# Attention over 16 heads: values as stationary operand in 64-column groups, two heads at a time

## The reference, cut to what matters

```python
def attend(q, k, v):                                   # 16 heads, dk 96, dv 64
    ...
    s = jnp.einsum('bqhd,bkhd->bhqk', qblk, k).astype(jnp.float32) * scale
    p = jax.nn.softmax(s, axis=-1).astype(v.dtype)
    return jnp.einsum('bhqk,bkhd->bqhd', p, v)
# o -> (tokens, 16*64) @ a_wo, times sigmoid(gate), added to the merged branches
```

## Time and profile before

| | |
|---|---|
| Median of 3 runs | 2784.48 us (2783.02 to 2785.2) |
| Profiled execution, its own time | 2785.75 us |
| Its span in the trace | 2783.9 us |
| Busy: TensorE, VectorE, ScalarE, GpSimd | 88%, 32%, 18%, 4% |
| Weight loads (beside the matmuls) | 54% |
| Mean granted TensorE clock | 0.927 of full |
| DMA | 440.60 MB, 158 GB/s over the span |

### The profile page before, as it was taken

One profiled execution on the slowest core, in us unless ns is written; L12 is line 12 of the kernel. 1 busy time (PEld: TensorE's weight loads), 2 busy tenths in 40 slices (PEclk: granted clock), 3 DMA queues, 4 the chain that ended last, 5 costly groups with the idle time before them and its releaser, 6 DMA issues. The chain is left out here.

```text
span 2783.9 us, 39618 instructions
## 1 busy us (share of the span) xinstructions
PE 2454.4 (88%) x16902; PEld 1508.4 (54%) x16902; DVE 893.8 (32%) x1492; ACT 510.1 (18%) x906; POOL 106.0 (4%) x74
## 2 busy tenths in 40 slices
PE   6999999889899969999479999997898999599893
PEld 3546654554576545555245476555545765455552
DVE  2255312431558130000113562224315661300002
ACT  1133202210223021010021241022102220201000
POOL 0000000000021000000000000001001110000000
PEclk8999999899989979999789999898999899699996
DMA  6321132114314277999353201411243222799972
GB/s 241 106 93 61 54 140 93 46 61 151 125 32 146 91 297 272 376 373 345 115 184 112 93 31 62 165 61 46 71 159 117 89 78 91 298 346 379 375 272 80
DMA packets 162338, 440.60 MB, mean 158 GB/s; under 512 B 10150, under 2 KB 50086, under 8 KB 153448
## 3 DMA queue, kind: packets, MB, share of 16 engines
q1 hardware_dynamic: 144360, 412.75, 40.6%
q10 hardware_dynamic: 14336, 12.59, 1.5%
q0 software_dynamic: 3456, 12.58, 1.2%
HBM read 400.38 MB, written 37.52 MB: 157 GB/s over the span
## 5 line engine op out<-in xcount | busy, mean ns | idle before, releaser
L293 PE MATMUL ps<-space 128*128 128x384 f32 (+3 forms) x1696 | 475.5, 433 | 14.9 <-DVE space L469 8.5
L293 PE MATMUL ps<-hT,space 128*128 128x384 f32 x1344 | 461.3, 504 | 27.3 <-ACT hT L407 12.1
L293 PEld LDWEIGHTS ps<-space 128*128 128x128 f32 x1696 | 300.1, 194 | 187.7 <-issue 48.4
L293 PEld LDWEIGHTS ps<-hT,space 128*128 128x128 f32 x1344 | 262.0, 197 | 213.4 <-issue 41.4
L1673 PE MATMUL ps<-space 128*32 128x256 f32 x6144 | 343.7, 384 | 1.7 <-ACT space L1783 1.5
L293 PE MATMUL ps<-space,hT 128*128 128x512 f32 x768 | 336.7, 599 | 3.8 <-PEq L1191 3.8
L1673 PEld LDWEIGHTS ps<-space 128*32 128x32 f32 x6144 | 201.9, 111 | 133.8 <-issue 12.6
L293 PEld LDWEIGHTS ps<-space,hT 128*128 128x128 f32 x768 | 146.9, 192 | 192.0 <-issue 191.4
L1694 PE MATMUL ps<-space 128*32 128x256 f32 x3072 | 184.2, 398 | 1.5 <-DVE space L1915 1.5
L325 PE MATMUL ps<-cst,space 128*128 128x128 f32 x492 | 84.6, 324 | 90.5 <-DVE space L1927 29.8
L1694 PEld LDWEIGHTS ps<-space 128*32 128x32 f32 x3072 | 100.9, 115 | 74.2 <-issue 15.8
(11 more groups left out here) (255 smaller groups left out, 2262.7 us busy)
## 6 DMA issues: line engine op xcount, KB each, us to landing
space<-in_e_w SPq DMA_DIRECT2D x96, 2048.0 KB, 15.2
space<-in_w_in SPq DMA_DIRECT2D x36, 2048.0 KB, 8.5
space<-in_w_ada SPq DMA_DIRECT2D x24, 2048.0 KB, 8.2
h_rows<-space SPq DMA_DIRECT2D x2, 6144.0 KB, 25.7
space<-h_rows SPq DMA_DIRECT2D x32, 384.0 KB, 17.9
y_rows<-mT ACTq DMA_DIRECT2D x128, 96.0 KB, 10.4
space<-in_a_wo SPq DMA_DIRECT2D x4, 2048.0 KB, 11.4
space<-in_b_wo SPq DMA_DIRECT2D x4, 2048.0 KB, 8.2
```

Source lines behind the costliest of these rows:

```text
L293: ins = pe.matmul(out, a, b, start=(i == 0), stop=(i == len(pairs) - 1))
```

## The change

In words:

- `weigh_values` works on a pair of heads j, once per six steps. The values are now the stationary operand (128 rows, 64 columns), head 2j in columns 0 to 63 and head 2j+1 in columns 64 to 127 of the array; the transposed probabilities move: 128 columns for the context tile, 256 for the two latent tiles. The output is feature-major. It alternates two PSUM banks.
- The probabilities are divided by the row sum before they are turned (`normalise`: reciprocal and scaling, VectorE), and TensorE's transposes wait for that instead of for exp.
- `probsT` becomes two buffers: `probsT_p` (context tile, two pairs) and `probsT_s` (latent tiles, one per head of a pair).
- The copies of the keys move from VectorE to ScalarE; ScalarE also copies each pair's output (`heads_out`) to `oT`, which now lies over the queries already used. `gT` moves to where the keys were.
- The gate block loses `to_features` for the attention's output and `features_dve` for it; `project_pe` waits for no copies there.

```diff
--- before.py
+++ after.py
@@ -124,7 +124,7 @@
         names = (
             "xin", "cond_clear", "cond_ready", "params_in", "cache_in", "squares_ready", "root_ready", "weighted",
             "h_ready", "cqn_ready", "ckvn_ready", "sq_ready", "summed", "stat_ready", "head_root", "rotary_in",
-            "nmax_ready", "abs_ready", "soft_ready", "logdecay_ready", "clamped_ready", "decay_ready",
+            "nmax_ready", "prob_ready", "abs_ready", "soft_ready", "logdecay_ready", "clamped_ready", "decay_ready",
             "qk_ready", "gla_state_in", "scaled_state", "state_ready", "o_ready", "conv_ready",
             "xbc_ready", "ssd_state_in", "diff_ready", "decayed_ready", "mask_ready", "xw_ready",
             "yoff_ready", "y_ready", "merged_ready", "chosen_ready", "zeros_ready", "zeroed", "rows_ready", "y_summed", "gated_ready", "y_scaled", "hidden_ready", "moe_ready", "stored",
@@ -472,9 +472,10 @@
 
         def project_pe(pe, chunks, key, src, tkey, between=None):
 
-            for t in range(NT):
-                for q in range(2):
-                    pe.wait_ge(*read((tkey, t, q)))
+            if tkey:
+                for t in range(NT):
+                    for q in range(2):
+                        pe.wait_ge(*read((tkey, t, q)))
             for i in range(2):
                 feature_major(pe, chunks[i], (key, i), src)
                 if between and i == 0:
@@ -554,16 +555,16 @@
         sq_x = carve(17920, KD, T)
         sq4 = m_flat[:, 0:QL // P * T].rearrange("p (a b) -> p a b", b=T)
         sq2 = m_flat[:, 1536:1536 + KVL // P * T].rearrange("p (a b) -> p a b", b=T)
-        o_tok = m_flat.rearrange("p (t d) -> p t d", d=D)
         head_qT = carve(20992, 2, T)
         head_kT = carve(21760, 2, T + P)
         probs = carve(22784, 3, T)
-        probsT = carve(23936, 2, T)
+        probsT_p = carve(23936, 2, 2, P)
+        probsT_s = carve(24768, 2, NT, 2 * P)
         nmax = carve(24704, 4)
         rsum = carve(24720, NT, H_A)
         mod_rows_a = carve(20992, 3, 512)
-        gT = [carve(T * k, T) for k in range(KD)]
-        oT = carve(4608, KD, T)
+        gT = [carve(4608 + T * k, T) for k in range(KD)]
+        oT = carve(0, NT * H_A * QK).rearrange("p (t j w) -> p j t w", t=NT, w=2 * QK)[:, :, :, 0:P]
 
         with nc.Fori(0, DEPTH) as l:
 
@@ -840,23 +841,23 @@
                     def turn_probs(i):
                         h, t = STEPS[i]
                         k0, k1 = KEYS[t]
-                        pe.wait_ge(*read(("s", i)))
+                        pe.wait_ge(*following(pe, "prob_ready"))
                         out = rotating(("pt", i))
                         for k in range(k1 - k0):
                             ins = pe.transpose(out[:, P * k:P * k + P], probs[:, i % 3, P * k:P * k + P], ident)
                         ins.then_inc(*makes(("pt", i)))
 
-                    def weigh_values(i):
-                        h, t = STEPS[i]
-                        k0, k1 = KEYS[t]
-                        if h % 8 == 0:
-                            claim(pe, ("pv", t, h // 8), B_PV + t)
-                        pe.wait_ge(*read(("pt", i)))
-                        c = V_A * (h % 8)
-                        ins = matmuls(pe, ps[:, B_PV + t, c:c + V_A],
-                                      [(probsT[:, i % 2, P * k:P * k + P], v_a[:, k0 + k, h, :]) for k in range(k1 - k0)])
-                        if h % 8 == 7:
-                            ins.then_inc(*makes(("pv", t, h // 8)))
+                    def weigh_values(j):
+                        out = claim(pe, ("pv", j), B_PV + j % 2)
+                        pe.wait_ge(*read(("pt", 2 * NT * j + 2 * NT - 1)))
+                        for i in range(2):
+                            pe.matmul(out[V_A * i:V_A * i + V_A, 0:P], v_a[:, 0, 2 * j + i, :], probsT_p[:, j % 2, i, :],
+                                      start=True, stop=True)
+                        for k in range(NT):
+                            for i in range(2):
+                                ins = pe.matmul(out[V_A * i:V_A * i + V_A, P:T], v_a[:, 1 + k, 2 * j + i, :], probsT_s[:, i, k, :],
+                                                start=(k == 0), stop=(k == NT - 1))
+                        ins.then_inc(*makes(("pv", j)))
 
                     head(0)
                     head(1)
@@ -867,8 +868,8 @@
                             head(next_head(i))
                         if 0 <= i < len(STEPS):
                             turn_probs(i)
-                        if i >= 1:
-                            weigh_values(i - 1)
+                        if i >= 1 and i % (2 * NT) == 0:
+                            weigh_values(i // (2 * NT) - 1)
 
                 @block.scalar
                 def _(act):
@@ -877,9 +878,20 @@
                         act.activation(head_qT[0:QK, h % 2, :], bank(("qT", h))[0:QK, 0:T], ACT.Copy).then_inc(*reads(("qT", h)))
                         act.wait_ge(*read(("qT", h)))
 
-                    queries(0)
-                    queries(1)
-                    for j in range(-AHEAD, len(STEPS)):
+                    def keys(h):
+                        act.wait_ge(*made(("kT", h)))
+                        act.activation(head_kT[0:QK, h % 2, :], bank(("kT", h))[0:QK, :], ACT.Copy).then_inc(*reads(("kT", h)))
+                        act.wait_ge(*read(("kT", h)))
+
+                    for h in range(2):
+                        queries(h)
+                        keys(h)
+                    def heads_out(j):
+                        act.wait_ge(*made(("pv", j)))
+                        act.activation(oT[:, j, :, :], quad(bank(("pv", j))[:, 0:T]), ACT.Copy).then_inc(*reads(("pv", j)))
+                        act.wait_ge(*read(("pv", j)))
+
+                    for j in range(-AHEAD, len(STEPS) + 2):
                         i = j + AHEAD
                         if i < len(STEPS):
                             h, t = STEPS[i]
@@ -892,36 +904,35 @@
                             act.activation(probs[:, i % 3, 0:n], s[:, 0:n], ACT.Exp, bias=nmax[:, i % 4:i % 4 + 1],
                                            accum_out=rsum[:, t, h:h + 1]).then_inc(*reads(("s", i)))
                             act.wait_ge(*read(("s", i)))
-                        if j >= 0 and next_head(j):
+                        if 0 <= j < len(STEPS) and next_head(j):
                             queries(next_head(j))
+                            keys(next_head(j))
+                        if j >= 2 and (j - 1) % (2 * NT) == 0:
+                            heads_out((j - 1) // (2 * NT) - 1)
 
                 @block.vector
                 def _(dve):
-                    def keys(h):
-                        dve.wait_ge(*made(("kT", h)))
-                        dve.tensor_copy(head_kT[0:QK, h % 2, :], bank(("kT", h))[0:QK, :]).then_inc(*reads(("kT", h)))
-                        dve.wait_ge(*read(("kT", h)))
-
                     def turned(i):
                         h, t = STEPS[i]
+                        dve.wait_ge(*made(("pt", i)))
+                        out = bank(("pt", i))
+                        if t == 0:
+                            ins = dve.tensor_copy(probsT_p[:, h // 2 % 2, h % 2, :], out[:, 0:P])
+                        else:
+                            ins = dve.tensor_copy(probsT_s[:, h % 2, :, P * (t - 1):P * t], quad(out[:, 0:T]))
+                        ins.then_inc(*reads(("pt", i)))
+                        dve.wait_ge(*read(("pt", i)))
+
+                    def normalise(i):
+                        h, t = STEPS[i]
                         n = P * (KEYS[t][1] - KEYS[t][0])
-                        dve.wait_ge(*made(("pt", i)))
-                        dve.tensor_copy(probsT[:, i % 2, 0:n], bank(("pt", i))[:, 0:n]).then_inc(*reads(("pt", i)))
-                        dve.wait_ge(*read(("pt", i)))
-
-                    def heads_out(t, g):
-                        dve.wait_ge(*made(("pv", t, g)))
-                        s = bank(("pv", t, g)).rearrange("p (h d) -> p h d", d=V_A)
-                        r = rsum[:, t, 8 * g:8 * g + 8]
+                        r = rsum[:, t, h:h + 1]
+                        dve.wait_ge(*read(("s", i)))
                         dve.reciprocal(r, r).then_inc(*counts("dve_step"))
                         dve.wait_ge(*counted("dve_step"))
-                        dve.tensor_tensor(o_tok[:, t, 512 * g:512 * g + 512].rearrange("p (h d) -> p h d", d=V_A),
-                                          s, over(r, V_A), ALU.mult).then_inc(*reads(("pv", t, g)))
-                        dve.wait_ge(*read(("pv", t, g)))
-
-                    keys(0)
-                    keys(1)
-                    for j in range(-AHEAD, len(STEPS) + 2):
+                        dve.tensor_scalar(probs[:, i % 3, 0:n], probs[:, i % 3, 0:n], r, None, ALU.mult).then_inc(*counts("prob_ready"))
+
+                    for j in range(-AHEAD, len(STEPS)):
                         i = j + AHEAD
```

(14 more changed lines are left out.)

## The result

The changed kernel takes 2790.2 us, the median of 11 runs (2783.4 to 2794.24), beside 2784.31 for the kernel before in the same job (11 runs): a ratio of 1.0022, 95% interval 1.0012 to 1.0033. It is not the gain of 0.3% that was predicted. The time lies inside the range, but that is luck, since the mechanism was not as forecast: the two stages were to give 7.8 us and took 1.6 us more than before in this profile.

What follows compares the result with a forecast made beforehand. TensorE was taken to bind before, hand-overs after. Per layer attention +1.9, gate stage -3.7, clock -1.3 and -0.8 made -3.9, -7.8 in all: 2785.75 to 2777.9 profiled, median 2776.7 us; range 2765 to 2796.

Steps and rivals of the forecast that it cites:

- The weighing: Attention, probabilities times values: two column groups run at once, 1.75 us a pair of heads against 2.82 before.
- rival 1: Attention's weighing: the two column groups don't overlap, 3.27 us for 1.75, +12.2 per layer, kernel 2801; chance 10%.
- The gate block: Gate stage: without 24 transposes and six copies the projection starts 3.7 us sooner; full clock there gives another -1.3 per layer.
- the cycle: Attention, steady pair of heads: hand-overs between engines bind, 9.60 us a pair for 9.23 before, +2.4 per layer.
- Rival 5: Gate stage gives nothing, the projection waiting for something else: 2787, no change; chance 2%.
- from there it is bound by its own work: 3.10: Last part of a pair in attention: from 6.50 us TensorE only does its own work, 3.10, closing at 9.60.
- step 6: Attention, following steps 0 to 5 of a pair: its scores wait for ScalarE's key copy until 6.50 us.
- time zero: Attention, start of counting a pair: when the probabilities of the even head's context step start to be turned.
- Rival 2: Attention: reciprocal and scaling each expose 0.2 to 0.3 us per hand-over; pair 10.2 (2784.5) or 10.7 (2791); chance 12%.
- the clock at the end of attention: Clock loss around the gate stage's start: idle gap shrinks from 2.64 to about 1.4 us, -0.8 per layer.
- the start: Attention's filling: first turning of probabilities waits for a scaling, behind which a maximum stands; +0.7 us per layer.
- Rival 4: Attention: the clock falls as more of TensorE's work is transposes; +5 us a pair, +80 in all, 2857; chance 3%.

Runs made afterwards that it cites:

- e9: Changed kernel with the weighing's matmuls ordered all of the even head, then all of the odd head, instead of alternating; ratio 1.0053 to the kernel before.
- e4: Kernel before with only the changed gate block (24 transposes and six copies left out); 3802.84 us, as other data gave later expert stages more work.
- e2: Changed kernel with the key copies moved back from ScalarE to VectorE; ratio 1.0041 to the kernel before.
- e3: Changed kernel without reciprocal and scaling of the probabilities, so the output is not normalised; 2766.06 us, ratio 0.9927 to the kernel before.
- e8: Changed kernel with query and key copies ahead of the exp on ScalarE, weighing behind the next scores, six rotating banks; ratio 1.0004 to the kernel before.
- e10: Changed kernel with only the weighing moved behind the next context step's scores; ratio 1.0062 to the kernel before.
- e1: Changed kernel with a sixth rotating PSUM bank, otherwise unused; ratio 0.9994 to the kernel before.
- e13: Changed kernel with 15 idle matmuls a layer in the waits of attention's last steps; 2783.74 us, ratio 0.9985 to the kernel before.
- e5: Changed kernel with PSUM's turn counter moved on by six claims, so later stages get their former banks; ratio 1.0022 to the kernel before.
- e14: Changed kernel with scores three steps ahead, earlier head turning and key copies, later weighing, six banks, 16 idle matmuls a layer; 2775.36 us, ratio 0.9960.

## Why the prediction was wrong, step by step

**Held.** The weighing: 1.66 for 1.75. Two groups of 64 run at once, as the four groups of 32 of the earlier trace rows had suggested; rival 1 (one after the other) is out, and e9 shows its price: 0.70 a pair when the program doesn't alternate. The Trainium skill (TensorE: Matmul & The Clock Gate, Measured speedup vs the span model) would have given an estimated 2.14 for a pair's weighing (1.9 and the 0.24 of changing shape) at its efficiency of three groups; the trace has no such loss with two (1.66). The gate block: -5.0 a layer for -3.7 and -1.3, shown alone by e4. The key copy on ScalarE is what the cycle waits for (0.80), and in the changed kernel's own order the cycle hangs on weighing, scaling and copy as laid out (e2, e3, e9). For other orders the same reckoning missed (e8, e10). Rival 5 is out.

**Failed, 1: the cycle, 9.88 for 9.60.** The step "from there it is bound by its own work: 3.10" is wrong. Up to the scores of step 6 the sum holds: 6.45 from time zero (267.99 to 274.44) for 6.50. Then the turning of the next context step waits for a bank, which is free when the exp of the following step has read it, and that exp waits for VectorE: 3.42 (274.44 to 277.86) for 3.10. I had followed data and engines, and not the banks. e1 takes this wait away and gets 9.67, as 6.65 and 3.01. Over 6.5 pairs it is +1.8 a layer. Rival 2 had a longer chain too, but by waits of reciprocal and scaling on VectorE, and of 0.6 a pair where 0.28 was measured; the bank stood in no rival. (TensorE's own work in a pair was given as 8.22; its parts add up to 8.17. Nothing hangs on it.)

**Failed, 2: the clock at the end of attention, -0.8 forecast.** It went the other way. I had reckoned that a shorter gap (2.64 before, 1.21 after) costs less. But the fall came ahead of that gap: in the last three steps the chain of scaling leaves TensorE waiting 1.25, 0.49 and 0.81 and busy for 3.2 of 6 us (the same stretch before: the earlier trace rows), and then the last weighing and the start of the gate projection run at 1.2 GHz. e13 shows what it cost: clock 1.00, and end and gate 61.4 a layer for 64.8 / 63.8, 3.3 and 2.4 us. Of the end's growth of 2.8 / 1.9 the chain (with whatever the fillers delay) is 1.2 (14.2 for 13.0; predicted 0.4) and the clock the rest; the gate stage would have given 5.4 instead of 3.7.

**Failed, 3, small: the start.** +1.1 in layer 0 for +0.7, with the clock at 0.72 over 238 to 244; +0.5 in layer 1.

**The sum.** In attention and gate +1.6 for -7.8, both layers: +3.9 by the heads (5.5 for 1.6), +3.9 by the end (4.7 for 0.8) and +1.6 by the clock gain that did not come (the -0.8 of the gate column, twice). The measured difference of the medians is 5.9, and where the other 4 us lie stays open. In the first pair of profiles the stages that nothing touched are longer (expert stages +4.4, gated linear attention +1.7), but one kernel's profiles differ there by 9. Some may lie in the two stages after all: e5's profile has +4.3 there and not +1.6. e5's median rules out the banks. The mirror image in e13 and e14 stays open as well: by their ratios they gain some 10 and 6 us on the kernels without fillers, and they show only 4.4 and 1.2 of it in the two stages.

**Rival 4** (the clock falls in the middle of attention) did not happen in the changed kernel: 1.00 over 250 to 300. It did in e2 and e10, for some us. By the Trainium skill (TensorE: Matmul & The Clock Gate, Part 4: PE-mode transpose) transposes would not hold the clock up; with a third of TensorE's pair in turnings it stayed full. What brings the fall is not settled. In e10 and at the end of attention TensorE stood idle between its groups, but in e8's layer 0 it was busy for even less (2.83 of 6 us) and the clock stayed at 1.00. And from the end of the last scores (312.04) to the last weighing (316.64) the changed kernel has only turnings on TensorE, so that rule may be at work there: the fillers of e13 are matmuls and fill both lacks at once. Fillers made of transposes would have told them apart; they were not tried.

## What to carry to other kernels

When work is taken off the engine that binds, lay out the new cycle with the buffers in it: who frees the PSUM bank that the next instruction claims is as much a link as who makes its data (9.60 became 9.88 by it). A cycle worked out for one order does not carry over to another: in none of the new orders did the pair come out as the reckoning had it. Where a stage's last steps are a chain between engines, count TensorE's clock into its price, and into that of the stage behind; a few idle matmuls in the waits were worth 0.4% and 0.2% here. Column groups overlap in full only if the program alternates them (1.66 for 2.37).

## What the runs showed of the hardware beyond that

- Two column groups of 64 run at the pace of one group: twelve halves over 256 columns begin and end within 1.47 us, about 0.22 a wave of two, where one half of the scores, 384 columns over the whole array, costs 0.35 (0.23 for 256 at that pace). In program order group by group they still overlap in part (2.37 for 1.66).
- The same instructions on the same chip, in two layers of one execution (e8), differ by 3.4 us at the end of attention and in the gate stage, with the granted clock at 1.00 in one and down to 0.54 in the other.
- The other stages, with not one instruction changed, took between 2411.2 and 2422.2 us over these profiles (without e4); between the two profiles of the changed kernel 8 of the 9 us lie in the expert stages. Why was not tried.
- On VectorE a reciprocal of 128x1 took 0.15 (I had taken 0.18) and a scaling of 128x384 in place 0.42, as taken.
